# A blocked triangular inverse on TensorE: 32x32 diagonal blocks in place of 64x64 matrices

## The reference, cut to what matters

```python
def step(S, inp):
    r_t, w_t, k_t, v_t, kk_t, a_t = inp
    sa = jnp.einsum('bhvk,bhk->bhv', S, -kk_t)
    S = (S * w_t[:, :, None, :] + sa[..., None] * (kk_t * a_t)[:, :, None, :]
         + v_t[..., None] * k_t[:, :, None, :])
    return S, jnp.einsum('bhvk,bhk->bhv', S, r_t)
# ... lax.scan(step, S0, over the 512 tokens), 4 heads of 64
```

## Time and profile before

| what | value |
|---|---|
| median of 3 runs | 1749.3 us (1746.36 to 1750.07) |
| the profiled execution's own time | 1742.45 us |
| its span on the core | 1740.7 us |
| PE busy | 1687.9 us, 97% of the span |
| PE weight loads | 1522.9 us |
| VectorE, ScalarE, GpSimd busy | 914.0, 646.1, 354.7 us |
| mean granted TensorE clock | 0.992 of full speed |

### The profile page before, as it was taken

The page is one execution under the profiler, slowest core; times in us unless marked ns, Lnnn a source line. Parts: engine busy times, 40 slices in busy tenths (PEclk is TensorE's granted clock), DMA queues, the critical chain, the costliest instruction groups (busy, mean ns, idle before and its releaser), DMA issues.

```text
span 1740.7 us, 32987 instructions
## 1 busy us (share of the span) xinstructions
PE 1687.9 (97%) x14287; PEld 1522.9 (87%) x14287; DVE 914.0 (53%) x1808; ACT 646.1 (37%) x1099; POOL 354.7 (20%) x466
## 2 busy tenths in 40 slices
PE   7999999989999899999999999999999999999997
PEld 3777779779988799999999998799769999999886
DVE  5457864463356645656560114898783565656002
ACT  3355532352155543222222224412783322222223
POOL 0001111002211022222222222343012222222221
PEclk9999999999999999999999999999999999999999
DMA  8532110238953278888888998699306889988896
GB/s 312 198 122 61 49 50 4 74 64 193 226 130 74 50 163 188 183 180 183 180 185 186 201 201 194 152 207 210 71 2 150 181 183 182 183 187 185 196 206 152
DMA packets 81648, 265.39 MB, mean 152 GB/s; under 512 B 11632, under 2 KB 15472, under 8 KB 81376
## 3 DMA queue, kind: packets, MB, share of 16 engines
q0 software_dynamic: 59040, 214.98, 58.1%
q1 hardware_dynamic: 18448, 42.52, 7.2%
q10 hardware_dynamic: 4016, 5.78, 1.2%
HBM read 251.44 MB, written 2.10 MB: 146 GB/s over the span
## 4 chain that ended last, share of the span: by engine, by line
PE 89%; DVE 5%; DMA 3%; ACT 2%; issue 1%; SPq 0%; ACTq 0%; POOL 0%; DVEq 0%
PE banks L668 21%; PE banks L669 21%; PE banks L670 21%; PE banks L2024 4%; PE banks L2026 3%; PE banks L2025 3%; PE banks L2319 3%; PE banks L805 1%; DMA w_lo<-in_weights 1%; PE banks L736 1%; PE banks L720 1%; PE banks L758 1%; PE banks L843 1%; DMA w_hi<-in_weights 1%; PE banks L1079 1%
## 5 line engine op out<-in xcount | busy, mean ns | idle before, releaser
L668 PE MATMUL banks<-hn_hi,w_hi 128*128 128x264 f32 (+2 forms) x2168 | 624.3, 288 | 4.7 <-DMA w_lo<-in_weights 4.0
L669 PE MATMUL banks<-hn_lo,w_hi 128*128 128x264 f32 (+2 forms) x2168 | 616.9, 285 | 0.0
L670 PE MATMUL banks<-hn_hi,w_lo 128*128 128x264 f32 (+2 forms) x2168 | 616.1, 284 | 0.0
L1216 ACT ACTIVATE w_lo<-w_hi 128x1024 fp32r<-128x1024 f32 x202 | 214.1, 1060 | 718.2 <-DMA w_hi<-in_weights 705.3
L668 PEld LDWEIGHTS banks<-hn_hi,w_hi 128*128 128x128 f32 x2168 | 408.9, 189 | 17.1 <-issue 12.2
L669 PEld LDWEIGHTS banks<-hn_lo,w_hi 128*128 128x128 f32 x2168 | 410.1, 189 | 0.6 <-issue 0.2
L670 PEld LDWEIGHTS banks<-hn_hi,w_lo 128*128 128x128 f32 x2168 | 408.0, 188 | 0.3
L1161 POOL DMA_DIRECT2D w_hi<-in_weights x205 | 113.5, 554 | 889.2 <-PE banks L670 803.5
L1168 POOL DMA_DIRECT2D w_lo<-in_weights x205 | 183.5, 897 | 160.7 <-ACT w_lo L1216 112.0
L668 PE MATMUL banks<-a_hi,w_hi 128*128 128x264 f32 (+1 forms) x506 | 160.5, 317 | 2.0 <-DVE u_in L1765 0.8
L669 PE MATMUL banks<-a_lo,w_hi 128*128 128x264 f32 (+1 forms) x506 | 160.7, 318 | 0.0
(11 more groups left out here) (453 smaller groups left out, 2730.9 us busy)
## 6 DMA issues: line engine op xcount, KB each, us to landing
w_hi<-in_weights POOLq DMA_DIRECT2D x205, 512.0 KB, 5.1
w_lo<-in_weights POOLq DMA_DIRECT2D x205, 512.0 KB, 7.2
ring<-in_weights SPq DMA_DIRECT2D x48, 512.0 KB, 4.6
arena<-arena ACTq DMA_DIRECT2D x64, 66.0 KB, 5.2
arena<-arena SPq DMA_DIRECT2D x64, 66.0 KB, 4.2
arena<-in_gate_w SPq DMA_DIRECT2D x8, 512.0 KB, 3.6
h<-in_xT SPq DMA_DIRECT2D x2, 1024.0 KB, 6.2
arena<-in_alibi SPq DMA_DIRECT2D x1, 1024.0 KB, 6.2
```

The source lines that it names most:

```text
L668: mm(o, w[0][:, j, :], x[0][:, k, lo:hi], start=first, stop=False)
L669: mm(o, w[0][:, j, :], x[1][:, k, lo:hi], start=False, stop=False)
L670: ins_ = mm(o, w[1][:, j, :], x[0][:, k, lo:hi], start=False, stop=last)
L1216: nc.scalar.activation(split_at(n)[1], split_at(n)[0].bitcast(F32), ACT.Copy, scale=-1.0).then_inc(S["w_negated"], 1)
```

## The change

Up to level 4 a 64x64 matrix has nothing outside its two 32x32 diagonal blocks. The changed kernel keeps only those: for each item and each of four partition quarters (two heads, two blocks) one 32x32 block. `r_x` is 16 x 2 x 32 columns, `r_t` is 32 columns an item, and a product is four matmuls of 32x32 on the four diagonal quarter-by-quarter tiles of the array (`four_blocks`), in place of two of 64x64. The transposes in `turn` stay as they are.

Level 5 joins the two 32x32 blocks of a head. Its two products are one 32x32 matmul a head, from one partition quarter to another. The full 64-column inverse goes to a new tile `r_xt`: VectorE fills its diagonal blocks by a product of X with a mask of halves, and copies the off-diagonal block from PSUM, 32 partitions at a time. Two small constants (`eye32`, `halfmask`) are made on VectorE ahead of the products' masks.

```diff
--- before.py
+++ after.py
@@ -223,12 +223,15 @@
     r_pr = cr.take(16, 4, 64)
     r_tok_at = cr.at
     r_tok = cr.take(16, 4, 64)
-    r_x = cr.take(16, 2, 64)
+    r_xt = cr.take(16, 64)
+    r_t1 = cr.take(16, 64)
     r_n = cr.take(2, 16, 64)
     cr.at = max(cr.at, g_end)
     r_e_flat = cr.take(3 * 2 * T1)
     r_el = cr.take(16)
     r_cols = cr.take(32)
+    eye32 = cr.take(32)
+    halfmask = cr.take(2)
     assert front + cr.at <= h1_tail_at
     cr.at = max(cr.at, h1_tail_at - front)
     r_zs = cr.take(2, T1)
@@ -245,13 +248,13 @@
     r_sq = r_bon
     r_mt = r_n[:, 0, :, :]
     r_s = r_n[:, 1, :, :]
-    r_t1 = r_x[:, :, 0, :]
     ck = Carve(hn_raw, KT * (T2 + 1))
-    r_t = ck.take(16, 64)
+    r_u = ck.take(16, 64)
+    r_t = r_u[:, :, 0:32]
     r_wt = ck.take(16, 64)
+    r_x = r_wt.rearrange("p m (a t) -> p m a t", a=2)
     r_wtt = ck.take(16, 64)
     r_ub = ck.take(16, 64)
-    r_u = r_t
     y1_buf = Carve(arena[:, front:ARENA], ARENA - front).take(KT, T1)
 
     rmask = first.enter_context(nc.sbuf_tensor("rmask", [P, 5 * 64], F32))
@@ -2350,6 +2353,13 @@
                                       src, rmask[:, 256:320])
             last.then_inc(S["r_tokps"], 1)
 
+        def four_blocks(out, lhs, rhs):
+
+            for b in range(4):
+                last = mm(out(slice(32 * b, 32 * b + 32)), lhs(slice(32 * b, 32 * b + 32), b % 2), rhs(slice(32 * b, 32 * b + 32), b % 2),
+                          start=True, stop=True)
+            return last
+
         def level_t(lv, i):
 
             if lv == 0:
@@ -2362,7 +2372,13 @@
                     pe.wait_ge(S["x_upd"], i + 1)
                 elif lv > 1 and c % 4 == 0:
                     pe.wait_ge(S["x_upd"], 2 + 4 * (lv - 2) + 2 * i + c // 4 + 1)
-                last = both_heads(lambda s: r_out(i, 0, c, s), r_n[:, lv % 2, m, :], r_x[:, m, 0, :] if lv else rmask[:, 256:320])
+                if lv < 5:
+                    last = four_blocks(lambda r: psum[r, 4 * i, 32 * c:32 * c + 32], lambda r, q: r_n[r, lv % 2, m, 32 * q:32 * q + 32],
+                                       lambda r, q: r_x[r, m, 0, :] if lv else rmask[r, 256 + 32 * q:288 + 32 * q])
+                else:
+                    for s in range(2):
+                        r, below = slice(64 * s, 64 * s + 32), slice(64 * s + 32, 64 * s + 64)
+                        last = mm(psum[below, 4 * i, 32 * c:32 * c + 32], r_n[r, lv % 2, m, 32:64], r_x[r, m, 0, :], start=True, stop=True)
             last.then_inc(S["r_tps"], 1)
 
         def level_x(lv, i):
@@ -2371,12 +2387,15 @@
             for c in range(8):
                 m = 8 * i + c
                 if lv < 5:
-                    both_heads(lambda s: psum[64 * s:64 * s + 64, 4 * i + 1 + c // 4, P * (c % 4):P * (c % 4) + 64], r_x[:, m, 1, :], r_t[:, m, :])
-                    last = both_heads(lambda s: psum[64 * s:64 * s + 64, 4 * i + 1 + c // 4, P * (c % 4) + 64:P * (c % 4) + P], r_t[:, m, :], r_x[:, m, 1, :])
+                    at = 64 * (c % 4)
+                    four_blocks(lambda r: psum[r, 4 * i + 1 + c // 4, at:at + 32], lambda r, q: r_x[r, m, 1, :], lambda r, q: r_t[r, m, :])
+                    last = four_blocks(lambda r: psum[r, 4 * i + 1 + c // 4, at + 32:at + 64], lambda r, q: r_t[r, m, :], lambda r, q: r_x[r, m, 1, :])
                     if c % 4 == 3:
                         last.then_inc(S["r_xps"], 1)
                 else:
-                    last = both_heads(lambda s: r_out(i, 1, c, s), r_t[:, m, :], r_x[:, m, 1, :])
+                    for s in range(2):
+                        above, r = slice(64 * s, 64 * s + 32), slice(64 * s + 32, 64 * s + 64)
+                        last = mm(psum[above, 4 * i + 1, 32 * c:32 * c + 32], r_t[r, m, :], r_x[r, m, 1, :], start=True, stop=True)
             if lv == 5:
                 last.then_inc(S["r_xps"], 1)
 
@@ -2398,17 +2417,17 @@
...
-                last = both_heads(lambda s: r_out(i, 0, c, s), r_x[:, m, 1, :], r_tok[:, m, 0, :])
+                last = both_heads(lambda s: r_out(i, 0, c, s), r_xt[:, m, :], r_tok[:, m, 0, :])
...
@@ -2694,7 +2713,13 @@
             for i in range(2):
                 if lv:
                     act.wait_ge(S["r_tps"], 2 * lv + i + 1)
-                    r_copy(r_t, i, 0).then_inc(S["r_tsb"], 1)
+                    if lv < 5:
+                        A(items(r_t, i), r_bank(i, 0)[:, 0:256].rearrange("p (u m) -> p u m", u=8), ACT.Copy).then_inc(S["r_tsb"], 1)
+                    else:
+                        for s in range(2):
+                            below = slice(64 * s + 32, 64 * s + 64)
+                            last = A(items(r_t, i)[below], r_bank(i, 0)[below, 0:256].rearrange("p (u m) -> p u m", u=8), ACT.Copy)
+                        last.then_inc(S["r_tsb"], 1)
                 if lv < 4:
                     r_tokens(2 * lv + i)
         for i in range(2):
@@ -3027,6 +3052,8 @@
         ve.wait_ge(S["r_sums"], 3)
         V.tensor_tensor(mix[:, 4:6, :], psum[:, 4:6, :], zv, ALU.mult).then_inc(S["r_inputs"], 1)
 
+        V.tensor_tensor(eye32, rmask[:, 256:288], rmask[:, 288:320], ALU.add)
+        V.tensor_reduce(out=halfmask, in_=rmask[:, 256:320].rearrange("p (a m) -> p a m", a=2), axis=mybir.AxisListType.X, op=ALU.add)
         masks = rmask[:, 0:256].rearrange("p (a m) -> p a m", a=1).to_broadcast([P, 2, 256])
         def masked(b):
             ve.wait_ge(S["r_prod"], b + 1)
@@ -3050,20 +3077,31 @@
         first_level(1)
         for i in range(2):
             ve.wait_ge(S["r_n0"], i + 1)
-            V.tensor_tensor(items(r_x, i)[:, :, 1, :], items(r_n[:, 0], i), eye64(8), ALU.add)
+            x, n0 = items(r_x, i), items(r_n[:, 0], i)
+            eyes = eye32.rearrange("p (a m) -> p a m", a=1).to_broadcast([P, 8, 32])
+            st.link(V.tensor_tensor(x[:, :, 1, :], n0[:, :, 0:32], n0[:, :, 32:64], ALU.add))
+            V.tensor_tensor(x[:, :, 1, :], x[:, :, 1, :], eyes, ALU.add)
             ve.wait_ge(S["r_tps"], i + 1)
-            V.tensor_tensor(items(r_x, i)[:, :, 0, :], r_bank(i, 0).rearrange("p (u m) -> p u m", u=8), eye64(8), ALU.add).then_inc(S["x_upd"], 1)
+            V.tensor_tensor(x[:, :, 0, :], r_bank(i, 0)[:, 0:256].rearrange("p (u m) -> p u m", u=8), eyes, ALU.add).then_inc(S["x_upd"], 1)
         for lv in range(1, 5):
             for i in range(2):
                 for b in range(2):
                     ve.wait_ge(S["r_xps"], 4 * (lv - 1) + 2 * i + b + 1)
                     ve.wait_ge(S["x_upd"], i + 1 if lv == 1 else 2 + 4 * (lv - 2) + 2 * i + b + 1)
                     x = r_x[:, 8 * i + 4 * b:8 * i + 4 * b + 4]
-                    V.tensor_tensor(x, x, r_bank(i, 1 + b).rearrange("p (u a m) -> p u a m", u=4, a=2), ALU.add).then_inc(S["x_upd"], 1)
+                    V.tensor_tensor(x, x, r_bank(i, 1 + b)[:, 0:256].rearrange("p (u a m) -> p u a m", u=4, a=2), ALU.add).then_inc(S["x_upd"], 1)
+        for i in range(2):
+            ve.wait_ge(S["x_upd"], 2 + 4 * 3 + 2 * i + 2)
+            st.did(V.tensor_tensor(items(r_xt, i).rearrange("p u (a m) -> p u a m", a=2),
+                                   items(r_x, i)[:, :, 1:2, :].to_broadcast([P, 8, 2, 32]),
+                                   halfmask.rearrange("p (u a o) -> p u a o", u=1, o=1).to_broadcast([P, 8, 2, 32]), ALU.mult))
+        st.settle()
         for i in range(2):
             ve.wait_ge(S["r_xps"], 16 + i + 1)
-            x = items(r_x, i)[:, :, 1, :]
-            V.tensor_tensor(x, x, r_bank(i, 1).rearrange("p (u m) -> p u m", u=8), ALU.add).then_inc(S["x_upd"], 1)
+            for s in range(2):
+                above = slice(64 * s, 64 * s + 32)
+                last = V.tensor_copy(items(r_xt, i)[above, :, 32:64], r_bank(i, 1)[above, 0:256].rearrange("p (u m) -> p u m", u=8))
+            last.then_inc(S["x_upd"], 1)
 
         def r_whole(i, b, n=8):
             return r_bank(i, b)[:, 0:64 * n].rearrange("p (u m) -> p u m", u=n)
```

More of the change, by code:

```diff
@@ L2404, in _ @@
                 m = 8 * i + c
-                last = both_heads(lambda s: r_out(i, 1, c, s), r_tok[:, m, 0, :], r_x[:, m, 1, :])
+                last = both_heads(lambda s: r_out(i, 1, c, s), r_tok[:, m, 0, :], r_xt[:, m, :])
             last.then_inc(S["r_wps"], 1)
@@ L2410, in _ @@
                 m = 8 * i + c
-                last = both_heads(lambda s: r_out(i, 3, c, s), r_x[:, m, 1, :], r_t1[:, m, :])
+                last = both_heads(lambda s: r_out(i, 3, c, s), r_xt[:, m, :], r_t1[:, m, :])
             last.then_inc(S["r_ups"], 1)
```

## The result

| | before | after |
| --- | --- | --- |
| median of 4 runs, us | 1747.8 (1745.8 to 1750.1) | 1774.9 (1767.8 to 1776.9) |
| profiled execution, its span, us | 1742.45, 1740.7 | 1767.75, 1766.0 |
| products of TensorE in the six levels and their transposes | 608 | 1024 |

The ratio is 1.0146, with a 95% interval of 1.0125 to 1.0168: slower, where 1740.1 us was forecast. An fp32 product is two weight loads and two matmuls, four instructions, so the levels have 4096 instructions after and 2432 before (waits not counted).

A forecast was written before the change was run, and what follows sets the result against it. TensorE was taken to bound the kernel, 44.56 us without a break. Terms 20.3 + 1.4 + 0.35 + 0.5 = 22.6 us against 31.7, 9.2 less, took the median of 1749.3 to 1740.1 us; range 1735 to 1767.

The forecast's parts named there:

- The pace of a record: In the levels, a 32x32 record costs 7.8 ns with four quarter tiles at once; bounds 7.8 and 29.2.
- The line through the tile widths: From measured full-width and 64-wide tiles, 113 and 58.3 ns, it gave 31 ns for a 32-wide tile.
- The levels at that pace: Levels 1 to 5 on TensorE at 7.8 ns a record, transposes as before: 20.3 us, against 31.7.
- Rival A: Floor under each TensorE record, 26 to 29 ns whatever the tile: slower, 1767 to 1772 us; chance 0.30.
- Two of its marks: Signs of a floor in the levels: X groups of 3.3 to 3.7 us, level windows of 11 to 13.
- a floor of 25 ns: The skill's start-to-start minimum for matmuls; if for all tiles together, 15.8 us more, 1765 us.
- Changes of shape: Between tile shapes on TensorE's path: 14 changes of 0.10 us, 1.4 us; between 0 and 2.8.
- VectorE, 0.35 and 0.5 us: 0.35 us for two constants ahead of the masks; 0.5 us for TensorE's wait for group 1's first X.
- The collision: Group 1's last two-input sum on VectorE falls into GpSimd's four masks, ending near 258.4; TensorE waits 0.5 us.
- Rival C: Chain of copies paces the levels, some 2.3 us each; with 0.2 more at levels 4 and 5, 1741; kept inside the forecast.
- level 5's copies: T goes out in two 32-partition copies a group; first X product waits 0.35, the second another 0.25: level 2.6 us.
- The time behind the levels: Behind the recurrence the saving arrives at the end; the half-clock stretch may move or vanish, worth 1.7 us either way.

The follow-up runs named there:

- run 1: The changed kernel with every product of levels 0 to 4 of the inverse in bf16: 1749.3 us, 1.0009 of before.
- run 2: The changed kernel with the T products of levels 0 to 4 made with 64x64 weights and 32 moving columns: 1766.2 us, 1.0114 of before.
- run 3: The changed kernel with 64 moving columns in place of 32 in the T products of levels 1 to 4: 1773.0 us, 1.0149 of before.
- run 4: The kernel before with level 5 alone as 32x32 blocks, two copies a group: 1745.8 us, 0.9997 of before.
- run 5: The changed kernel with two long-fulfilled waits ahead of each of the 832 quarter-array products of levels 0 to 4: 1839.2 us, 1.0522 of before.
- run 6: The kernel before with one X product in levels 1 to 4, its transpose made by VectorE, 64x64 tiles kept: 1740.4 us, 0.9971 of before.
- run 7: The kernel of run 6 with no product in level 0, the first X a VectorE transpose: 1742.5 us, 0.9983 of before.
- run 9: The changed kernel with two unused 128x256 fp32 matmuls ahead of each T group of levels 1 to 5: 1780.2 us, 1.0170 of before.
- run 10: The changed kernel with T by 64x64 weights and one X product in 32x32 blocks, transposed by VectorE: 1749.5 us, 1.0009 of before.
- run 12: The kernel of run 6 with level 5 as 32x32 blocks and one copy of T a group: 1739.6 us, 0.9960 of before.
- run 8: Separate kernel of matmul streams only: 768 fp32 32x32 products over four tiles, 42.1 us; fifth stream, the same beside 12 MB of loads, 53.8; as a loop, 18.3.

## Why the prediction was wrong

| run | instructions | packets x 3.59 us | levels measured | PE busy |
| --- | --- | --- | --- | --- |
| before | 2432 | 34.1 | 37.1 | 35.7 |
| after | 4096 | 57.4 | 57.0 | 36.7 |
| 1, bf16 | 2432 | 34.1 | 36.6 | 25.4 |
| 2, T by 64x64 | 3456 | 48.5 | 51.4 | 39.1 |
| 3, twice the columns in T | 4096 | 57.4 | 58.2 | 41.1 |
| 4, last level alone | 2432 | 34.1 | 36.4 | 34.7 |
| 5, with waits (832 of them counted) | 4928 | 69.1 | 124.2 | 123.9 |
| 6, one X product, 64x64 | 1920 | 26.9 | 29.6 | 28.3 |
| 7, level 0 without products | 1792 | 25.1 | 32.4 | 28.7 |
| 9, with fillers | 4176 | 58.6 | 64.0 | 49.0 |
| 10, both savings, 32x32 | 2432 | 34.1 | 36.7 | 30.8 |
| 12, run 6 and level 5 | 1920 | 26.9 | 28.6 | 27.1 |

The third column is no full account of a level: it leaves out that some instructions are there at the start, and the first waits for VectorE (1.3 us before). It bounds the changed kernel and runs 1, 2, 3 and 10. The kernel before and runs 4, 6 and 12 are at the pace of their 64x64 records, run 5 at that of its waits; run 7 also waits 3.6 us for VectorE.

- *The pace of a record, 7.8 ns:* right, within a tenth, for a record whose instructions have arrived (8.6 ns in the T group at 258.15; at half clock, from 301.04 on, (1.92 - 0.24)/127 = 13 ns). The line through the tile widths in the earlier trace rows was sound.
- *The levels at that pace, 20.3 us:* this is the step that failed. It multiplied all 1664 records by the pace of one, "with nothing left for an issue limit". There is a limit, not of a record but of the supply: 14.0 ns an instruction as a mean over a packet. Levels 1 to 5, forecast at 20.3 us, took 51.9, and with level 0 the 16 packets of 3.59 us are 57.4 us against 57.0 measured. The rows were too short to meet it: 32 records are 64 instructions, well inside one packet. What came near it stood in front of me: 7.47 us a level for 512 instructions is 3.74 us a packet, 4% over the supply's 3.59. TensorE was busy all the time and stood a few per cent from another limit, one that the change moves in proportion to its count.
- *Rival A, 0.30:* right in size and wrong in mechanism. Its 25.9 to 29.2 ns a record gave 1767 to 1772 us, since the supply's 28 ns is in that range; measured 1774.9. Two of its marks came as sums over the pauses: level windows of 11.6, 11.8 and 13.1 us, and level 1's two X groups in 6.8 us, 3.4 each. The third did not: a T group without a pause in it takes 0.74 us, not 1.6 to 1.9. The range of 1735 to 1767 stopped at A's lower end.
- *By the Trainium skill,* TensorE: Matmul & The Clock Gate, section "Wait — 56ns, not 53.3ns?", a floor of 25 ns gave an estimate of 1765 us. For four tiles at once the traces disagree: 8.6 ns inside a packet. For one tile alone, run 8 has 51 ns (39.2 us for 768 records) at a clock of 0.54, so it shows no value at 2.4 GHz.
- *Changes of shape, 1.4 us:* not measured by themselves. The streams have none and show the pauses all the same.
- *VectorE, 0.35 and 0.5 us:* right. The two constants took 0.18 and 0.21 us. The collision came as foretold: the two-input sum at 258.37 took 1.37 us beside GpSimd, T of level 1's second group started at 260.23, and TensorE waited 0.7 us for VectorE in front of level 1's two T groups, where it waited 0.3 before.
- *Rival C and level 5's copies:* hidden. Level 5 goes by its packets too, and run 4 shows that part neutral. There TensorE waited 0.3 us for the copies of T, where the forecast had 0.35 and 0.25.
- *The time behind the levels:* a saving was to arrive unchanged, and the half-clock stretch was worth 1.7 us. The loss grew there by 3.3 us (15.90 and 21.62 us at clocks of 0.85 and 0.88, against 13.69 and 20.56 at 1.00 and 0.95). That the pauses brought this half clock is not shown. Run 6, whose levels had no pauses, kept 13.69 and took 21.1, but run 4, whose levels had none either and ran at 1.00, had clocks of 0.89 from 290 to 310 us and 0.76 from 310 to 330, and its profiled execution took 1752.1 us, 6 over its median. Run 9 kept TensorE busier and won nothing.

## What to carry to other kernels

Count TensorE's instructions, not only its columns. Where a long stretch of code asks for an instruction more often than every 14 ns, the fetch of code is the bound, and smaller tiles lose. An fp32 product of 64x64x64 in two tiles takes four instructions in 58.4 ns, 14.6 each, and just stays clear of it. The sign is "issue" between matmuls on one line, exactly 128 records apart, and a busy instruction queue at even distances. What helped here is fewer instructions for the same result: one product and a VectorE transpose in place of two products (run 10 against 2), wider weights over block-diagonal data (run 2), bf16 where it is exact enough (run 1), or a loop that stays within two packets (384 instructions is the longest tried). None of the versions in 32x32 blocks beat the kernel before; the ones that did, runs 6, 7 and 12, keep 64x64 tiles and have fewer products.

## What the hardware showed that I had not expected

- A packet of 256 instructions takes 3.6 to 3.7 us with idle DMA queues and (337.06 - 312.83)/4 = 6.06 us beside loads at 420 GB/s. The timeline of run 8's fifth stream, and the GB/s over its 53.8 us, in 40 slices:

```profile
312.83 1.93 PE L53 MATMUL banks<-x 32*32 32x32 f32 x128 [3.56 <-issue]
...
337.06 1.93 PE L53 MATMUL banks<-x 32*32 32x32 f32 x128 [4.27 <-issue]
```

```profile
GB/s 67 251 410 410 416 440 416 410 446 403 428 434 397 434 434 410 422 422 403 422 440 385 428 263 73 0 12 0 0 12 0 12 0 0 12 0 0 12 0 12
```

- A loop in TensorE's program is cheap beside a fetch: 16 turns of 192 instructions ran 768 products in 18.3 us, 42.1 unrolled. A turn cost some 0.3 us above its records (1.14 us less 96 x 8.6 ns), against 2.7 us for the fetch of 192 instructions at 14 ns.
- A wait on a semaphore that is long fulfilled is free if it rides on a product. As an instruction of its own it adds 81 ns to code that the supply holds, in the kernel and in the stream alike, and 102 ns (132 less 30) to the products' own pace at half clock.
- TensorE without a single pause can still be granted 1.2 GHz: in the stream on one 32x32 tile, and in that with two waits a product, at a clock of 0.54.
